# Moving four weight-remainder splits from VectorE to GpSimd, and re-ordering the depthwise convolution on VectorE

## The chip, the cores and the metric

The kernel runs on one core of a Trainium2 chip. The metric is the device time of one execution in microseconds; the table below gives the median of three.

## The reference, cut to what matters

A four-layer model (retention, conformer convolution, stick-breaking attention, retention, each followed by a squared-ReLU MLP) feeds a two-layer hybrid model, on one sequence of 256 tokens with 1024 channels in float32. Two stages matter here.

The conformer mixer, once in the program:

```
h = rms_norm(x)                               # 256 x 1024
a, b = split(h @ pw1_w + pw1_b)               # two halves of 1024
u = a * sigmoid(b)                            # the gated product
y[t, c] = dw_b[c] + sum_m dw_w[m, c] * u[t - 30 + m, c]     # 31 taps per channel
y = silu(layer_norm(y)) @ pw2_w + pw2_b ;  x = x + y
```

The attention of a hybrid layer, twice in the program: 16 heads of 64, scores over 256 keys with a bias, a softmax with a sink, probabilities times values, then `@ w_attn_out`, gates, and `@ w_o`.

## The kernel before, in words

Channels lie on partitions: a 256 x 1024 activation is 8 tiles of 128 x 256. Every product with a weight is made of three TensorE products (`three`, L679): the operand is split into a rounded part `hi` and the remainder `lo`, and hi*hi, hi*lo and lo*hi are summed. Weights stream from memory in units of 128 x 4096 (1 MB), 404 pieces of half a unit in all, through two buffers each of `raw`, `w_hi` and `w_lo` (unit u uses buffer u % 2). For each piece ScalarE rounds `w_hi <- raw` (L1099), VectorE computes `w_lo <- raw - w_hi` (L1507), and TensorE waits for `lo_done`. The helpers `ahead` and `next_unit` on both engines call these splits one unit ahead of use. SyncE loads unit u into `raw[u % 2]` once unit u - 2 is split (`lo_done`).

Each engine runs its own program in written order, and semaphores tie them together.

The conformer uses units 32 to 37. Units 32 to 35 give the two halves of pw1: one unit gives one PSUM pair with two tiles of `a` (columns 0 to 511) and two of `b` (columns 512 to 1023). ScalarE copies the `a` tiles with their bias into `C_U` (L1287) and writes sigmoid of the `b` tiles to `C_GATE` (L1290); that releases the PSUM pair. VectorE multiplies two tiles at once in place (`gated`, L1833). The depthwise convolution has eight tiles. VectorE makes tiles 0, 1, 2, 4 and 6: one scalar_tensor_tensor per tap, `y = u_shifted * w + y`, of 128 x 256 (L1795 for the tile pairs 0/1 and 2/4; L1813 for tile 6, which alternates between two accumulators and adds them at the end, L1818). TensorE makes tiles 3, 5 and 7 as 31 matmuls each with diagonal matrices (L869), which GpSimd builds (`diagonals`, L581: 62 of them early, the last 31 after `w_hi` of unit 35 has begun, because they lie in a buffer that is busy until then). Then TensorE takes the mean and the variance over channels (L888, L894), and units 36 and 37 are pw2.

The order on VectorE inside a convolution uses `link_late`: an instruction signals `vec`, and the next one waits only for the one before the last. Its elsewhere-used sister `link` waits for the instruction itself.

In a hybrid layer's attention, for each of 8 head groups VectorE adds the bias to scores (L2043), takes a maximum (L2049), and, after ScalarE's exponentials (L1443), normalises (L2060); TensorE transposes (L1033), ScalarE evacuates (L1449), TensorE multiplies with the values (L1042), VectorE evacuates (L1879). GpSimd fetches the bias tiles by DMA as `released` allows. The unit whose split this change touches there is the first of `w_attn_out`, called ATTN_OUT below; ScalarE rounds it at `j == 6`, VectorE subtracts it before `outputs(7)`.

Of the kernel before, what the change touches and what calls it, by code (L numbers as in the profile page):

```python
# [314 lines left out]
def build_program(nc, stream, columns, x_in, rows, tables, rel_bias, bias_rows, scratch, out):  # L315
# [6 lines left out]
    with ctx:  # L322
# [60 lines left out]
        conv_gated = sem("conv_gated")  # L383
# [60 lines left out]
        C_GATE = tiles(gate[:].rearrange("p b n -> p (b n)"))  # L444
# [33 lines left out]
        TABLES_BIAS, TABLES_RET, TABLES_CONV, TABLES_SB, TABLES_HYBRID = 6, (6, 16), 7, 12, (18, 20)  # L478
        CONV_FIRST = 16 + 2 * FFN1_CHUNKS
# [55 lines left out]
        def _(pool):  # L535
# [47 lines left out]

            retention(0)
# [12 lines left out]
            pool.wait_ge(hi_done, 2 * (CONV_FIRST + 3) + 1)  # L597
            diagonals(2)
            region_free()
# [43 lines left out]
        def _(pe):  # L643
# [215 lines left out]
            def conformer():  # L859
                convolved = {}  # L860

                def convolve(n):
# [3 lines left out]
                    pe.wait_ge(conv_gated, k // 2 + 1)  # L866
# [8 lines left out]
                unit_f(middle=turn_first)  # L875
                unit_f()
                convolve(0)
                unit_f()
                convolve(1)
                convolve(2)  # L880
# [208 lines left out]
        def _(act):  # L1089
# [184 lines left out]
            def conformer():  # L1274
# [7 lines left out]
                for i in range(4):  # L1282
                    o, done, slot = result(i == 0)
                    if i == 0:
                        act.wait_ge(zeroed, ZEROED_CONV)
                    for t in range(2):
                        run(C_U[:, 2 * i + t, TAPS - 1:UW], o[:, SEQ * t:SEQ * (t + 1)], ACT.Identity,  # L1287
                            bias=colv("pw1_b", 2 * i + t))
                    for t in range(2):
                        last = run(C_GATE[:, 2 * i + t, :], o[:, 512 + SEQ * t:512 + SEQ * (t + 1)],  # L1290
                                   ACT.Sigmoid, bias=colv("pw1_b", KT + 2 * i + t))
                    last.then_inc(done, 1)
# [96 lines left out]
            def hybrid(layer):  # L1389
# [65 lines left out]
                for j in range(8):  # L1455
# [3 lines left out]
                    if j == 6:  # L1459
# [38 lines left out]
        def _(dve):  # L1498
# [278 lines left out]
            def conformer(layer):  # L1777
                def link_late(ins):

                    ins.then_inc(vec, 1)  # L1780
                    dve.wait_ge(vec, S.due("vec") - 1)

                def convolve(first, second, between={}):

                    for m in range(TAPS):
                        if m in between:
                            between[m]()
                        for k in (first, second):
                            if m == TAPS - 1 and k == second:
                                dve.wait_ge(vec, S.seen["vec"])  # L1790
# [11 lines left out]
                def convolve_one(k):  # L1802

                    for m in range(TAPS):
                        dst = C_Y[:, k, :] if m % 2 == 0 else C_M
# [8 lines left out]
                        if m < TAPS - 1:  # L1814
                            link_late(ins)
                        else:
# [3 lines left out]
                def gated(i):  # L1820

                    if i == 0:
                        ahead(S.u + 1)
                        S.u += 1
                        ahead(S.u + 1)
                        use(False)
                    else:
                        ahead(S.u + 1)
                        S.u += 1
                        use()  # L1830
                    await_drained(S.p - 1)
                    two = slice(2 * i, 2 * i + 2)
                    tt(C_U[:, two, TAPS - 1:UW], C_U[:, two, TAPS - 1:UW], C_GATE[:, two, :],  # L1833
                       ALU.mult).then_inc(conv_gated, 1)
                    dve.wait_ge(conv_gated, i + 1)
                    if i == 2:
                        use(False)

                gated(0)
# [13 lines left out]
                ahead(CONV_FIRST + 4)  # L1853
# [10 lines left out]
                ahead(CONV_FIRST + 5)  # L1864
                S.u += 2
                add_bias(C_B)

# [84 lines left out]
            def hybrid(layer):  # L1952
# [126 lines left out]
                ahead(S.u + 1)  # L2079
# [3 lines left out]
                S.u += 1  # L2083
                rest_hid(4)
                for i in range(2):
# [57 lines left out]
```

## Time and profile before

| | us |
|---|---|
| median of 3 runs | 2527.19 (2526.38 to 2528.08) |
| the profiled execution | 2527.19 |
| its span, first to last instruction | 2525.4 |
| TensorE busy | 2416.1 (96%) |
| VectorE busy | 1500.9 (59%) |
| ScalarE busy | 1141.8 (45%) |
| GpSimd busy | 147.4 (6%) |

Rows of a timeline begin with the start in us from the span's start, then the time from the first start to the last end of the merged instructions, the engine, the line, the operation, output and inputs with shapes, and the count; brackets hold the idle time just before and who ended it. DVE is VectorE, ACT ScalarE, POOL GpSimd, PE TensorE.

### The profile page before, as it was taken

The numbers are of one execution on the slowest core, as the hardware profiler recorded it, in microseconds if no ns is written. First come the engines' busy times: TensorE is split into PE (matmuls) and PEld (weight loads), VectorE is DVE, ScalarE is ACT, GpSimd is POOL, SyncE is SP. The second block draws the span as 40 slices with busy tenths as digits, with TensorE's granted clock in tenths as the row PEclk, the third lists the DMA queues.
The fourth block names the chain that finished last, engine by engine and source line by source line (L and its number), as shares of the span: only waits on it lengthen the run. The fifth ranks groups of instructions, "written<-read, shape, count | busy, mean of one in ns | idle before, by whom it ended". The sixth has DMA issues, their size and how long they took to land.

```text
span 2525.4 us, 35292 instructions
## 1 busy us (share of the span) xinstructions
PE 2416.1 (96%) x14772; PEld 2157.7 (85%) x14772; DVE 1500.9 (59%) x1481; ACT 1141.8 (45%) x1127; POOL 147.4 (6%) x189
## 2 busy tenths in 40 slices
PE   7999999979999899999999999998999999989998
PEld 6787998869987789877789889998899899978997
DVE  6666556955466665586665565466644564586454
ACT  5444444144447654364444434354433443454443
POOL 0000170410000000000000000000000000010000
PEclk9999999989999999999999999999999999999999
DMA  6444654124544154545364434352454444423443
GB/s 255 175 183 173 231 202 168 67 83 193 199 166 167 67 192 173 197 163 188 142 238 179 183 143 194 151 192 80 163 200 195 179 176 175 176 94 136 193 167 123
DMA packets 68434, 424.38 MB, mean 168 GB/s; under 512 B 10848, under 2 KB 11136, under 8 KB 22496
## 3 DMA queue, kind: packets, MB, share of 16 engines
q1 hardware_dynamic: 58752, 399.83, 40.9%
q0 software_dynamic: 9568, 22.90, 2.9%
q8 instruction: 87, 1.43, 0.2%
q14 instruction: 27, 0.22, 0.0%
HBM read 421.60 MB, written 5.28 MB: 169 GB/s over the span
## 4 chain that ended last, share of the span: by engine, by line
PE 86%; DVE 8%; ACT 3%; issue 1%; DMA 0%; POOL 0%; DVEq 0%; ACTq 0%; POOLq 0%
PE pair L680 18%; PE pair L682 18%; PE pair L681 18%; PE acc L680 9%; PE acc L681 9%; PE acc L682 9%; DVE work L1795 2%; PE pair L717 1%; DVE w_lo L1507 1%; PE pair L1042 1%; DVE work L2043 1%; ACT work L1166 1%; PE pair L984 1%; DVE small L2049 1%; ACT act_hi L1148 0%
## 5 line engine op out<-in xcount | busy, mean ns | idle before, releaser
L1507 DVE TENSOR_TENSOR w_lo<-raw,w_hi 128x2048 fp32r<-128x2048 f32 (+1 forms) x404 | 859.7, 2163 | 258.1 <-ACT w_hi L1099 257.1
L1099 ACT ACTIVATE w_hi<-raw 128x2048 fp32r<-128x2048 f32 (+1 forms) x404 | 713.0, 1806 | 152.8 <-PE acc L682 132.6
L680 PE MATMUL pair<-act_hi,w_hi 128*128 128x256 f32 x2496 | 708.5, 284 | 2.5 <-DVE w_lo L1507 2.5
L682 PE MATMUL pair<-act_hi,w_lo 128*128 128x256 f32 x2496 | 706.3, 283 | 0.0
L681 PE MATMUL pair<-act_lo,w_hi 128*128 128x256 f32 x2496 | 706.3, 283 | 0.0
L680 PEld LDWEIGHTS pair<-act_hi,w_hi 128*128 128x128 f32 x2496 | 478.9, 192 | 5.2 <-issue 2.8
L681 PEld LDWEIGHTS pair<-act_lo,w_hi 128*128 128x128 f32 x2496 | 478.9, 192 | 2.3
L682 PEld LDWEIGHTS pair<-act_hi,w_lo 128*128 128x128 f32 x2496 | 478.8, 192 | 0.0
L680 PE MATMUL acc<-w_hi,hid_hi 128*128 128x512 f32 x848 | 334.7, 395 | 4.9 <-DVE hid_lo L1560 4.9
L681 PE MATMUL acc<-w_lo,hid_hi 128*128 128x512 f32 x848 | 331.0, 390 | 0.0
L682 PE MATMUL acc<-w_hi,hid_lo 128*128 128x512 f32 x848 | 330.5, 390 | 0.0
L680 PE MATMUL pair<-w_hi,act_hi 128*128 128x512 f32 (+1 forms) x576 | 225.8, 392 | 10.4 <-DVE w_lo L1507 6.3
L682 PE MATMUL pair<-w_hi,act_lo 128*128 128x512 f32 (+1 forms) x576 | 222.1, 386 | 0.0
L681 PE MATMUL pair<-w_lo,act_hi 128*128 128x512 f32 (+1 forms) x576 | 221.9, 385 | 0.0
L680 PEld LDWEIGHTS acc<-w_hi,hid_hi 128*128 128x128 f32 x848 | 159.8, 188 | 38.1 <-DVE hid_lo L1560 5.4
L682 PEld LDWEIGHTS acc<-w_hi,hid_lo 128*128 128x128 f32 x848 | 159.6, 188 | 33.9
L681 PEld LDWEIGHTS acc<-w_lo,hid_hi 128*128 128x128 f32 x848 | 159.9, 189 | 32.3 <-issue 1.4
L1650 DVE TENSOR_TENSOR val<-gate 128x1024 f32<-128x1024 f32 x32 | 39.3, 1227 | 210.2 <-ACT gate L1195 210.2
L1195 ACT ACTIVATE gate<-pair 128x1024 f32<-128x1024 f32 x32 | 32.9, 1027 | 247.5 <-PE pair L682 239.5
L680 PEld LDWEIGHTS pair<-w_hi,act_hi 128*128 128x128 f32 x576 | 109.0, 189 | 36.0 <-issue 9.9
L682 PEld LDWEIGHTS pair<-w_hi,act_lo 128*128 128x128 f32 x576 | 108.8, 189 | 21.9
L681 PEld LDWEIGHTS pair<-w_lo,act_hi 128*128 128x128 f32 x576 | 109.0, 189 | 21.3 <-issue 0.7
(212 smaller groups left out, 2588.0 us busy)
## 6 DMA issues: line engine op xcount, KB each, us to landing
raw<-weights SPq DMA_DIRECT2D x356, 1024.0 KB, 6.7
raw<-weights SPq DMA_DIRECT2D x48, 512.0 KB, 6.3
work<-bias_scratch POOLq DMA_DIRECT2D x32, 192.0 KB, 3.6
bias_scratch<-bias_rows POOLq DMA_DIRECT2D x4, 1024.0 KB, 22.6
work<-ret_gn_w POOLq DMA_DIRECT2D x8, 256.0 KB, 5.4
work<-ret_gn_b POOLq DMA_DIRECT2D x8, 256.0 KB, 5.8
work<-table_pool POOLq DMA_DIRECT2D x2, 1024.0 KB, 5.6
work<-table_decay POOLq DMA_DIRECT2D x2, 768.0 KB, 6.9
```

Of the source, the lines that this page charges most:

```text
L680: mm(o, a_hi, b_hi, start=start, stop=False)
L681: mm(o, a_hi, b_lo, start=False, stop=False)
L682: return mm(o, a_lo, b_hi, start=False, stop=stop)
L717: last = tr(o[:, P * k:P * (k + 1)], xs[:, a, P * k:P * (k + 1)], ident[:])
L984: last = mm(o[:, (k % 4) * SEQ:(k % 4 + 1) * SEQ], H_UP[:, s, k * P:(k + 1) * P], H_POOL[:, k // 2, s, :], start=s == 0, stop=s == 1)
L1042: last = mm(o[:, 512 * i:512 * i + SEQ], H_V[:, s, P * (j // 4):P * (j // 4) + P], H_PT[:, j % 2, i, s, :], start=s == 0, stop=s == 1)
L1099: run(w_hi[slot][:, part], raw[slot][:, part], ACT.Copy).then_inc(hi_done, 1)
L1166: run(xs[:, a, :], x[:, a, :], ACT.Square, scale=D ** -0.5, accum_out=ss[:, a:a + 1]).then_inc(ss_ready, 1)
L1195: run(gate[:, slot, :], o[:], ACT.Relu).then_inc(done, 1)
L1507: tt(w_lo[slot][:, part], raw[slot][:, part], w_hi[slot][:, part].bitcast(F32), ALU.subtract).then_inc(lo_done, 1)
L1650: tt(val[:, S.c % 2, :], gate[:, slot, :], gate[:, slot, :], ALU.mult).then_inc(value_ready, 1)
L1795: ins = stt(C_Y[:, k, :], C_U[:, k, m:m + SEQ], colv("dw_w", KT * m + k), C_Y[:, k, :], ALU.mult, ALU.add)
```

## The change

1. GpSimd gets `split_low`, the same subtraction as L1507, and runs it for units 35, 36 and 37 of the conformer (35 ahead of the last 31 diagonals, 36 and 37 behind them) and for ATTN_OUT in each hybrid layer (behind the last bias tile). VectorE drops these, and instead waits for `lo_done` at the end of the conformer and of the attention. On ScalarE the rounding of ATTN_OUT moves from `j == 6` to `j == 1`.
2. In the conformer ScalarE no longer copies the `a` tiles. VectorE makes the gated product straight from PSUM, one scalar_tensor_tensor per tile, `(a + bias) * gate`, and this now releases the PSUM pair. TensorE's diagonal convolutions wait for that release.
3. On VectorE tiles 0 and 1 are made one after the other with the two-accumulator form, tiles 2 and 4 as a pair, tile 6 as before; `link_late` goes, and the engine waits (`link`) for the second of every two instructions.

```diff
+            def split_low(u):
+                slot = u % 2
+                for piece in range(2):
+                    part = place_of(u, piece)
+                    pool.wait_ge(lo_done, 2 * u + piece)
+                    pool.wait_ge(hi_done, 2 * u + 1 + piece)
+                    nc.gpsimd.tensor_tensor(w_lo[slot][:, part], raw[slot][:, part], w_hi[slot][:, part].bitcast(F32),
+                                            ALU.subtract).then_inc(lo_done, 1)
...
-            pool.wait_ge(hi_done, 2 * (CONV_FIRST + 3) + 1)
+            split_low(CONV_FIRST + 3)
             diagonals(2)
+            split_low(CONV_FIRST + 4)
+            split_low(CONV_FIRST + 5)
...
                     bias_tile(j)
+                split_low(ATTN_OUT[layer])
...
-                    pe.wait_ge(conv_gated, k // 2 + 1)
+                    await_drained(unit_use)
...
-                    for t in range(2):
-                        run(C_U[:, 2 * i + t, TAPS - 1:UW], o[:, SEQ * t:SEQ * (t + 1)], ACT.Identity,
-                            bias=colv("pw1_b", 2 * i + t))
...
-                    if j == 6:
+                    if j == 1:
                         ahead(S.u + 1)
...
-                            if m < TAPS - 1:
-                                link_late(ins)
-                            else:
-                                ins.then_inc(conv_ready, 1)
+                        if m < TAPS - 1:
+                            link(ins)
+                        else:
+                            ins.then_inc(conv_ready, 2)
...
+                    for t in range(2):
+                        last = stt(C_U[:, 2 * i + t, TAPS - 1:UW], o[:, SEQ * t:SEQ * (t + 1)],
+                                   colv("pw1_b", 2 * i + t), gate[:, slot, SEQ * t:SEQ * (t + 1)], ALU.add, ALU.mult)
+                    last.then_inc(done, 1)
...
-                gated(0)
-                ahead(CONV_FIRST + 2)
-                convolve(0, 1, {12: lambda: gated(1), 13: lambda: ahead(CONV_FIRST + 3)})
-                gated(2)
-                convolve(2, 4, {10: lambda: gated(3)})
+                gated(0)
+                convolve_one(0)
+                gated(1)
+                convolve_one(1, lambda: gated(2))
+                convolve(2, 4, lambda: gated(3))
                 convolve_one(6)
...
-                ahead(S.u + 1)
                 outputs(7)
...
                 rest_hid(4)
+                dve.wait_ge(lo_done, 2 * S.split)
```

VectorE in the conformer, from the first gated product on, before (C_U, C_Y and the accumulators all lie in `work`):

```order
L1833 TENSOR_TENSOR work<-work,gate 128x2x256
L1792 TENSOR_SCALAR work<-work,cols 128x256 x2
L1795 SCALAR_TENSOR_TENSOR work<-work,cols 128x256 x22
L1833 TENSOR_TENSOR work<-work,gate 128x2x256
L1795 SCALAR_TENSOR_TENSOR work<-work,cols 128x256 x2
L1507 TENSOR_TENSOR w_lo<-raw,w_hi 128x2048 x2
L1795 SCALAR_TENSOR_TENSOR work<-work,cols 128x256 x36
L1833 TENSOR_TENSOR work<-work,gate 128x2x256
L1792 TENSOR_SCALAR work<-work,cols 128x256 x2
L1795 SCALAR_TENSOR_TENSOR work<-work,cols 128x256 x18
L1507 TENSOR_TENSOR w_lo<-raw,w_hi 128x2048 x2
L1833 TENSOR_TENSOR work<-work,gate 128x2x256
```

and now (line numbers of the changed kernel):

```order
L1832 SCALAR_TENSOR_TENSOR work<-pair,cols,gate 128x256 x2
L1815 TENSOR_SCALAR work<-work,cols 128x256
L1817 TENSOR_SCALAR work<-work,cols 128x256
L1819 SCALAR_TENSOR_TENSOR work<-work,cols 128x256 x29
L1822 TENSOR_TENSOR work<-work 128x256
L1832 SCALAR_TENSOR_TENSOR work<-pair,cols,gate 128x256 x2
L1815 TENSOR_SCALAR work<-work,cols 128x256
L1817 TENSOR_SCALAR work<-work,cols 128x256
L1819 SCALAR_TENSOR_TENSOR work<-work,cols 128x256 x14
L1832 SCALAR_TENSOR_TENSOR work<-pair,cols,gate 128x256 x2
L1819 SCALAR_TENSOR_TENSOR work<-work,cols 128x256 x15
L1822 TENSOR_TENSOR work<-work 128x256
```

The two pairs of `w_lo` subtractions are gone from between the taps, the gated products read the PSUM pair, and tiles 0 and 1 come one after the other.

GpSimd around the diagonals, before:

```order
L581 TENSOR_SCALAR work<-ident,cols 128x128 x83
L581 TENSOR_SCALAR val<-ident,cols 128x128 x10
L539 DMA work<-table_sb_mask 128x384
```

and now:

```order
L580 TENSOR_SCALAR work<-ident,cols 128x128 x62
L591 TENSOR_TENSOR w_lo<-raw,w_hi 128x2048 x2
L580 TENSOR_SCALAR work<-ident,cols 128x128 x21
L580 TENSOR_SCALAR val<-ident,cols 128x128 x10
L591 TENSOR_TENSOR w_lo<-raw,w_hi 128x2048 x4
L538 DMA work<-table_sb_mask 128x384
```

Six subtractions of 128 x 2048 come to this engine here, two ahead of the last 31 diagonals and four behind them.

## Rows read from the trace of the kernel before

**Rows 1.** The page's head: span, busy time of each engine.
```profile
span 2525.4 us, 35292 instructions
PE 2416.1 (96%) x14772; PEld 2157.7 (85%) x14772; DVE 1500.9 (59%) x1481; ACT 1141.8 (45%) x1127; POOL 147.4 (6%) x189
```

**Rows 2.** Chain that ended last, conformer: start us, us, what.
```profile
431.49 0.85 ACT gate L1290 x2
432.37 0.70 DVE work L1833
...
444.06 4.50 DVE w_lo L1507 x2
448.56 14.84 DVE work L1795 x36
...
472.30 4.40 DVE w_lo L1507 x2
...
494.64 11.49 DVE work L1813 x29
506.16 0.43 DVE work L1818
```

**Rows 3.** Timeline of VectorE, end of the conformer.
```profile
493.97 0.41 DVE L1809 TENSOR_SCALAR work<-work,cols 128x256 f32<-128x256 f32 x1
...
528.50 4.49 DVE L1507 TENSOR_TENSOR w_lo<-raw,w_hi 128x2048 fp32r<-128x2048 f32 x2
```

**Rows 4.** Timeline of VectorE, hybrid layer: the short convolution with `link`.
```profile
1488.22 0.62 DVE L1966 TENSOR_SCALAR work<-work,cols 128x256 f32<-128x256 f32 x2
1488.88 1.80 DVE L1968 SCALAR_TENSOR_TENSOR work<-work,cols 128x256 f32<-128x256 f32 x4
```

**Rows 5.** Timeline of ScalarE, conformer.
```profile
429.35 0.84 ACT L1287 ACTIVATE work<-pair,cols 128x256 f32<-128x256 f32 x2 [2.00 <-PE pair L799]
...
436.56 3.73 ACT L1099 ACTIVATE w_hi<-raw 128x2048 fp32r<-128x2048 f32 x2
...
484.91 0.48 ACT L1280 ACTIVATE work<-pair,cols 128x256 f32<-128x256 f32 x1 [8.22 <-PE pair L869]
498.30 0.48 ACT L1280 ACTIVATE work<-pair,cols 128x256 f32<-128x256 f32 x1 [12.91 <-PE pair L869]
```

**Rows 6.** The instructions of GpSimd's L581: duration ns min/median/max, first and last start.
```profile
L581 POOL TENSOR_SCALAR work<-ident,cols x83: 595/601/5034, 307.4 to 462.9; 128x128 f32<-128x128 f32 x83
```

**Rows 7.** Timeline of GpSimd and VectorE around one such meeting.
```profile
344.94 3.45 POOL L581 TENSOR_SCALAR work<-ident,cols 128x128 f32<-128x128 f32 x1
344.40 2.47 DVE L1507 TENSOR_TENSOR w_lo<-raw,w_hi 128x2048 fp32r<-128x2048 f32 x1 [0.49 <-ACT w_hi L1099]
331.97 2.29 DVE L1507 TENSOR_TENSOR w_lo<-raw,w_hi 128x2048 fp32r<-128x2048 f32 x1 [1.94 <-ACT w_hi L1099]
```

**Rows 8.** GpSimd by line and form: count, busy us, mean ns, idle before.
```profile
L546 POOL MEMSET work<- 64x2048 f32 x6 | 10.9, 1809 | 513.6 <-DVE small L1578 513.4
```

**Rows 9.** Timeline of GpSimd, conformer.
```profile
438.58 25.21 POOL L581 TENSOR_SCALAR work<-ident,cols 128x128 f32<-128x128 f32 x21 [73.86 <-ACT w_hi L1099]
463.78 8.48 POOL L581 TENSOR_SCALAR val<-ident,cols 128x128 f32<-128x128 f32 x10
```

**Rows 10.** Timelines of GpSimd and VectorE, first hybrid layer's attention.
```profile
1713.16 1.07 POOL L539 DMA_DIRECT2D work<-bias_scratch  x2 [4.42 <-DVE small L1578]
1714.71 0.18 DVE L2059 RECIPROCAL small<-small 128x4 f32<-128x4 f32 x1
1714.92 1.23 DVE L2060 TENSOR_TENSOR work<-work,small 128x1024 f32<-128x1024 f32 x1
1719.52 0.16 DVE L2050 TENSOR_TENSOR small<-small,work 128x4 f32<-128x4 f32 x1
1735.85 4.49 DVE L1507 TENSOR_TENSOR w_lo<-raw,w_hi 128x2048 fp32r<-128x2048 f32 x2
```

**Rows 11.** Waits between 1694 and 1750 us: who for whom, us, times, longest.
```profile
PE pair L1033 <- DVE work L2060: 7.2, 5, 2.7
PE pair L680 <- issue: 1.2, 1, 1.2
```

More of the change, by code:

```diff
@@ L382, in build_program @@
         conv_ready = sem("conv_ready")
-        conv_gated = sem("conv_gated")
         centred = sem("centred")
@@ L443, in build_program @@
         C_Y, C_SQ = tiles(work[:, 2304:4352]), tiles(work[:, 0:2048])
-        C_GATE = tiles(gate[:].rearrange("p b n -> p (b n)"))
         C_MEAN = work[:, 6400:6528]
@@ L478, in build_program @@
         TABLES_BIAS, TABLES_RET, TABLES_CONV, TABLES_SB, TABLES_HYBRID = 6, (6, 16), 7, 12, (18, 20)
+        ATTN_OUT = [n_units - 2 * FFN2_CHUNKS * (2 - layer) - HYBRID_UNITS * (1 - layer) - 4 for layer in range(2)]
         CONV_FIRST = 16 + 2 * FFN1_CHUNKS
@@ L875, in conformer @@
                 unit_f(middle=turn_first)
+                use_1 = S.p - 1
                 unit_f()
-                convolve(0)
+                use_2 = S.p - 1
+                convolve(0, use_1)
                 unit_f()
-                convolve(1)
-                convolve(2)
+                use_3 = S.p - 1
+                convolve(1, use_2)
+                convolve(2, use_3)
                 o = open_pair()
@@ L1283, in conformer @@
                     o, done, slot = result(i == 0)
-                    if i == 0:
-                        act.wait_ge(zeroed, ZEROED_CONV)
                     for t in range(2):
-                        run(C_U[:, 2 * i + t, TAPS - 1:UW], o[:, SEQ * t:SEQ * (t + 1)], ACT.Identity,
-                            bias=colv("pw1_b", 2 * i + t))
-                    for t in range(2):
-                        last = run(C_GATE[:, 2 * i + t, :], o[:, 512 + SEQ * t:512 + SEQ * (t + 1)],
+                        last = run(gate[:, slot, SEQ * t:SEQ * (t + 1)], o[:, 512 + SEQ * t:512 + SEQ * (t + 1)],
                                    ACT.Sigmoid, bias=colv("pw1_b", KT + 2 * i + t))
-                    last.then_inc(done, 1)
+                    last.then_inc(gate_ready, 1)
                     if i == 2:
@@ L1777, in conformer, with convolve @@
             def conformer(layer):
[L1778 to L1783, printed above, removed]
+                def convolve(first, second, middle):
                     for m in range(TAPS):
-                        if m in between:
-                            between[m]()
+                        if m == 26:
+                            middle()
                         for k in (first, second):
-                            if m == TAPS - 1 and k == second:
-                                dve.wait_ge(vec, S.seen["vec"])
                             if m == 0:
@@ L1796, in convolve, with convolve_one @@
                                           C_Y[:, k, :], ALU.mult, ALU.add)
-                            if m < TAPS - 1:
-                                link_late(ins)
-                            else:
-                                ins.then_inc(conv_ready, 1)
-                def convolve_one(k):
+                        if m < TAPS - 1:
+                            link(ins)
+                        else:
+                            ins.then_inc(conv_ready, 2)
+                def convolve_one(k, middle=None):
                     for m in range(TAPS):
+                        if m == 16 and middle is not None:
+                            middle()
                         dst = C_Y[:, k, :] if m % 2 == 0 else C_M
@@ L1813, in convolve_one @@
                             ins = stt(dst, src, w, dst, ALU.mult, ALU.add)
-                        if m < TAPS - 1:
-                            link_late(ins)
-                        else:
+                        if m % 2 or m == TAPS - 1:
                             link(ins)
@@ L1820, in gated @@
                 def gated(i):
+                    o, done, slot = result(i == 0)
                     if i == 0:
-                        ahead(S.u + 1)
[L1824 to L1830, printed above, removed]
+                        S.split += 3
+                    S.g += 1
+                    dve.wait_ge(gate_ready, S.g)
+                    for t in range(2):
+                        last = stt(C_U[:, 2 * i + t, TAPS - 1:UW], o[:, SEQ * t:SEQ * (t + 1)],
+                                   colv("pw1_b", 2 * i + t), gate[:, slot, SEQ * t:SEQ * (t + 1)], ALU.add, ALU.mult)
+                    last.then_inc(done, 1)
                     await_drained(S.p - 1)
[L1832 to L1835, printed above, removed]
                     if i == 2:
                         use(False)
+                dve.wait_ge(zeroed, ZEROED_CONV)
                 gated(0)
-                ahead(CONV_FIRST + 2)
-                convolve(0, 1, {12: lambda: gated(1), 13: lambda: ahead(CONV_FIRST + 3)})
-                gated(2)
-                convolve(2, 4, {10: lambda: gated(3)})
+                convolve_one(0)
+                gated(1)
+                convolve_one(1, lambda: gated(2))
+                convolve(2, 4, lambda: gated(3))
                 convolve_one(6)
@@ L1852, in conformer @@
                 release_centred()
-                ahead(CONV_FIRST + 4)
                 o, done = fetch_pair()
@@ L2078, in hybrid @@
                 outputs(6)
-                ahead(S.u + 1)
                 outputs(7)
@@ L2083, in hybrid @@
                 S.u += 1
+                S.split += 1
                 rest_hid(4)
+                dve.wait_ge(lo_done, 2 * S.split)
                 for i in range(2):
```

3 lines of the change are left out of this document (1 added, 2 removed).

## The prediction

> **What bounds the kernel now.** I read the page's head first: TensorE is busy 96% of a span of 2525.4 us and VectorE 59% [rows 1]. So work taken from VectorE gains only where TensorE waits for VectorE. The chain of waits says where the changed code is such a place. In the conformer the chain leaves TensorE when ScalarE ends the first sigmoids and stays on VectorE from 432.37 to 506.59 us: gated products, taps, and the two pairs of `w_lo` subtractions that stand between the taps [rows 2]. There every microsecond on VectorE is one of the kernel. TensorE's own last diagonal convolution has ended when ScalarE evacuates it at 498.30 [rows 5], 8 us ahead of VectorE. In the attention of the hybrid layers TensorE waits five times for VectorE's normalisation, 7.2 us in one layer [rows 11]; so up to about 1730 us VectorE is the path there too.
>
> **The change on VectorE and ScalarE alone.** Four terms, all in the conformer.
>
> (a) ScalarE's two copies ahead of the first sigmoids took 0.84 us [rows 5]; without them the first gated product starts so much earlier: -0.8.
>
> (b) Four gated products took 0.70 us each with a gap of about 0.03 [rows 2]: 2.9. Now each is two scalar_tensor_tensors of 128 x 256. The linked pair of the hybrid layer is the nearest row: four in two linked pairs take 1.80 us [rows 4]. One instruction lasts 0.48 and its neighbour starts 0.40 behind it (11.49 us for 29, [rows 2]), so a pair lasts 0.88 and the next pair starts at 1.80 - 0.88 = 0.92. Four at 0.92 are 3.7: +0.8. The PSUM source may cost some hundredths.
>
> (c) Two pairs of subtractions leave the path: -(4.50 + 4.40) = -8.9 [rows 2]. The third pair, at 528.50 [rows 3], lies beside the matmuls of unit 36, which run until unit 37 is wanted, and is worth nothing.
>
> (d) The links. Before, 36 taps took 14.84, 0.412 each, and 29 took 11.49, 0.396 each [rows 2]. Tiles 0, 1, 2 and 4 are 120 taps and 4 first products: 120 x 0.41 + 1.4 = 50.6. Tile 6 runs from 493.97 to 506.59 [rows 2, 3]: 12.6. Together 63.2. Now a pair costs 0.92 for two taps. A single tile is 0.66 for its two tensor_scalars (1488.22 to 1488.88, [rows 4]), 14 pairs, one lone linked tap at 0.52 and the final addition at 0.43: 14.5. Three such are 43.5. Tiles 2 and 4 are 0.66 + 30 x 0.92 = 28.3. Together 71.8: +8.6.
>
> The sum of (a) to (d) is -0.3: what the subtractions give back, the waits take. Here the Trainium skill says otherwise. Its page "VectorE: DVE Perf Modes", section "The DRAIN you can't avoid", holds that a semaphore after each of a chain of operations costs nothing extra. This trace does not agree: 0.92 for a linked pair against 2 x 0.40 without the close wait [rows 2, 4]. By that rule (d) would be only the two additions, +0.9, and the sum -8.0.
>
> Does anything else become late? TensorE's convolutions now start after VectorE's gated products 1, 2 and 3. Without further delays product 1 comes at 431.5 + 0.9 + 14.5 = 447, product 3 at about 487, and the last diagonal convolution, 13.4 us long (484.91 to 498.30, [rows 5]), would end near 501, 6 us ahead of VectorE. The diagonals it needs end at 472.3 before [rows 9] and some 9 us later now, still ahead of 487.
>
> **The subtractions on GpSimd.** No row shows a GpSimd subtraction, so I bound it. Below: a memset of 2048 columns, one stream, is 1.81 us [rows 8]. Above: a tensor_scalar of 128 columns has a median of 0.60 [rows 6], and sixteen of them are 9.6. The memset is the nearer row, since start-up weighs most in a short instruction. If the two reads share one way in, it is 2 x 1.8 = 3.6; with the write not overlapped 5.4. I take the middle, 4.5.
>
> The Trainium skill has this very operation in "GPSIMD Engine Reference", section "Performance versus the Vector engine": 4497 ns for a tensor_tensor of 2048 float32. No run here shows it yet; the sum would be the same.
>
> The question is what VectorE does meanwhile. A GpSimd tensor_scalar of 0.60 us has a maximum of 5.03 [rows 6]. One took 3.45, from 344.94 on, while VectorE ran the subtraction that starts at 344.40 and the one behind it [rows 7]. So GpSimd stands still for whole VectorE instructions that read two operands from SBUF. It goes the other way as well: this VectorE subtraction took 2.47 against 2.29 for one on its own [rows 7]. That is 0.18 us, about what reading 128 columns takes. It looks as if the two engines take turns by instruction, not by element. If so, GpSimd's 2048 columns hold VectorE for nearly their whole length, and the taps, which read `C_U` and the accumulator, are stopped. Close waits leave VectorE without an instruction at the end of each pair, so GpSimd gets its turn within a microsecond.
>
> The rule in the Trainium skill is the same: "SBUF — State Buffer", section "Who interferes with whom", says that whoever comes first, VectorE with two SBUF inputs or GpSimd reading SBUF, has the shared ports for the whole instruction. The rows on which I rely are those above.
>
> (e) Conformer: 4.5 less the 0.2 that VectorE has free between pairs is 4.3 for each of 6 pieces: +25.8. All six fall on the path. ScalarE has the halves of unit 35 ready about 437.5 and 439.5 ([rows 5], less what it saves), so GpSimd subtracts in tile 0. The diagonals follow: 33.7 us before, one 4.5 us standstill in it [rows 9]; now 29. So units 36 and 37 come between about 477 and 496, in tiles 2 and 4. VectorE then ends near 506.6 - 0.3 + 25.8 = 532, and the last diagonal convolution, held by product 3, near 528 to 530, a slower clock after its wait counted in.
>
> (f) Attention, twice. GpSimd's last bias fetch is issued by 1714.2 [rows 10], and the first piece begins reading near 1714.7, in the reciprocal (one input) just ahead of the normalisation, which reads two SBUF operands [rows 10]. That waits 4.2. The second piece gets its turn after it, at about 1720.3, runs beside a copy and an addition that read PSUM and a reduction of one input (about 3.4 us), and holds the next small tensor_tensor about 1.1: together 5.3. Two layers: +10.6. The bounds are 2.1 (both pieces after a normalisation) and 8.6 (both ahead) a layer. Dropping VectorE's pair at 1735.85 [rows 10] gives nothing: TensorE is then in a weight unit and next waits 1.2 us for a PSUM buffer [rows 11]. Rounding earlier on ScalarE delays one group of exponentials by 3.4 us, which VectorE wants 4 us later: nothing.
>
> Sum: -0.3 + 25.8 + 10.6 = +36.1. The profiled execution took 2527.2 us, 1.8 more than its span and equal to the median, so the forecast is 2563. With the bounds of 1.8 and 9.6 for a piece, (e) runs from +9.6 to +56, and the whole from about 2538 to 2600; close to the middle I hold 3.8 to 5.4 a piece, 2554 to 2575 for this case.
>
> **Rivals.**
>
> *Shared by element.* VectorE's second operand gets every other turn while GpSimd reads. A tap reads 256 columns in some 0.28 of its 0.40 us (2048 take 2.2, [rows 2]); at half speed a pair goes from 0.92 to about 1.45, and a piece costs about 2.2. Conformer +13, attention +3: 2543. For it: the 0.18 is small. Against: GpSimd got nothing for 3 and 5 us, which sharing would not do.
>
> *VectorE always goes first.* GpSimd fills the gaps and VectorE loses only what it lost to the diagonals, 0.412 against 0.396 a tap. This ends on the other side, not slower: -0.3 + 1 = 2528. The place is the taps; it decides as long as a piece, stretched to about 10 us, still lets the diagonals end by 488 and unit 37 be split by 533. For it: 36 taps beside diagonals lost only 0.6 us [rows 2]. Against: a diagonal reads only 128 columns, so it fits in a gap, and the 0.18.
>
> *Links for nothing*, as by the skill's rule, and no stop: 2527.2 - 8.0 = 2519. The row of 1.80 speaks against it [rows 4].
>
> *A much longer GpSimd piece*, near the upper bound, with stops: 2590 or more.
>
> **How the numbers follow.** Stopped for whole instructions: 0.60, at 2563. Shared: 0.18, at 2543. VectorE first: 0.17, at 2528. Links for nothing: 0.03. Long piece: 0.02. The first case lies likeliest, so 2563. Stretching the first case by half its own width again and taking in the second, but leaving out the other three, gives 2531 to 2584 for 8 in 10. A measurement here tells 0.2%, 5 us, from no change. Faster: 0.03; within it: 0.15, nearly all of "VectorE first"; slower: 0.82.
>
> **What would show it.** Taps that read SBUF stretched from 0.48 to over 4 us, six times in the conformer and about twice in each attention, would show (e) and (f). GpSimd's L591 near 4.5 us would show the price. Linked pairs at 0.92 show (d). TensorE idle between its second and third diagonal convolution shows what waits. If taps stay at 0.48 during L591, I am wrong, and the time is near 2528; if they come to 0.7 or 0.8, it is sharing.

## The result and the profile after

The changed kernel takes 2570.20 us (median of 4 runs, 2569.77 to 2570.93) against 2527.64 (4 runs, 2526.38 to 2528.29): ratio 1.0169, 95% interval 1.0151 to 1.0187. It is 42.6 us slower. The forecast was +36.1. The head of the profile's page, to be held against [rows 1]:

```profile
span 2569.0 us, 35304 instructions
PE 2421.5 (94%) x14772; PEld 2162.4 (84%) x14772; DVE 1530.4 (60%) x1477; ACT 1137.2 (44%) x1119; POOL 180.5 (7%) x199
```

The span grew by 43.6 us and TensorE's busy time by only 5.4, so TensorE waits more. VectorE is busy 29.5 us longer although ten subtractions of 2.3 us have left it: what grew is the length of other instructions. GpSimd's subtraction and VectorE's taps, by line (duration in ns, least, median, most; first and last start):

```profile
L591 POOL TENSOR_TENSOR w_lo<-raw,w_hi x10: 4508/4617/4883, 437.6 to 2279.7; 128x2048 fp32r<-128x2048 f32 x10
...
L1819 DVE SCALAR_TENSOR_TENSOR work<-work,cols x87: 472/485/4816, 431.6 to 531.5; 128x256 f32<-128x256 f32 x87
...
L1799 DVE SCALAR_TENSOR_TENSOR work<-work,cols x60: 471/484/4824, 472.6 to 517.5; 128x256 f32<-128x256 f32 x60
```

A tap's median is what it was, and its longest is as long as a whole GpSimd instruction. The timeline of VectorE in the conformer (answers [rows 2, 3]; L1832 gated product, L1819 and L1799 taps, L1822 addition):

```profile
429.95 0.88 DVE L1832 SCALAR_TENSOR_TENSOR work<-pair,cols,gate 128x256 f32<-128x256 f32 x2
...
431.58 22.43 DVE L1819 SCALAR_TENSOR_TENSOR work<-work,cols 128x256 f32<-128x256 f32 x29
...
456.26 7.02 DVE L1819 SCALAR_TENSOR_TENSOR work<-work,cols 128x256 f32<-128x256 f32 x14
...
464.22 7.25 DVE L1819 SCALAR_TENSOR_TENSOR work<-work,cols 128x256 f32<-128x256 f32 x15
...
472.62 39.89 DVE L1799 SCALAR_TENSOR_TENSOR work<-work,cols 128x256 f32<-128x256 f32 x50
...
531.98 0.42 DVE L1822 TENSOR_TENSOR work<-work 128x256 f32<-128x256 f32 x1
```

Tile 1's 29 taps take 14.3 us (7.02 for 14 and 7.25 for 15); tile 0's, with the same work, take 22.4. The 50 taps at 472.62 would be 23 us at 0.92 a pair and take 39.9. GpSimd in the same stretch (answers [rows 9]):

```profile
437.56 9.62 POOL L591 TENSOR_TENSOR w_lo<-raw,w_hi 128x2048 fp32r<-128x2048 f32 x2 [73.14 <-ACT w_hi L1115]
447.16 14.07 POOL L580 TENSOR_SCALAR work<-ident,cols 128x128 f32<-128x128 f32 x21
...
473.19 9.55 POOL L591 TENSOR_TENSOR w_lo<-raw,w_hi 128x2048 fp32r<-128x2048 f32 x2 [5.42 <-ACT w_hi L1115]
485.05 9.37 POOL L591 TENSOR_TENSOR w_lo<-raw,w_hi 128x2048 fp32r<-128x2048 f32 x2 [2.31 <-ACT w_hi L1115]
```

The six pieces lie exactly where the taps are long. The chain of waits puts them side by side, pair by pair:

```profile
437.07 0.89 DVE work L1819 x2
...
437.99 9.48 DVE work L1819 x2
...
447.50 0.89 DVE work L1819 x2
...
484.88 5.17 DVE work L1799 x2
490.08 5.03 DVE work L1799 x2
```

One pair holds both pieces of unit 35: its first tap waits for the first piece, its second for the second. VectorE's convolution ends at 532.40 instead of 506.59, and pw2 starts at 549.95 instead of 525.57: +24.4.

In each attention both pieces meet VectorE's smallest operations (answers [rows 10]):

```profile
1738.65 4.75 DVE L2050 TENSOR_TENSOR small<-small,work 128x4 f32<-128x4 f32 x1
1743.44 0.17 DVE L2051 TENSOR_SCALAR small<-small 128x4 f32<-128x4 f32 x1
1743.64 4.34 DVE L2052 TENSOR_TENSOR small<-work,small 128x4 f32<-128x4 f32 x1
```

```profile
1737.78 1.07 POOL L538 DMA_DIRECT2D work<-bias_scratch  x2 [4.42 <-DVE small L1589]
1738.86 9.10 POOL L591 TENSOR_TENSOR w_lo<-raw,w_hi 128x2048 fp32r<-128x2048 f32 x2
```

L2050 and L2052 read two operands from SBUF each. An operation of 4 columns that takes 0.16 us [rows 10] takes 4.75. L2051 between them reads one operand and takes its usual time; but it starts at 1743.44, just as the second piece does (1743.45), so it may simply have slipped in between. TensorE's waits in the two stretches (432 to 560 us, and 1725 to 1775, which answers [rows 11]):

```profile
PE pair L882 <- DVE work L1832: 27.2, 2, 17.9
```

```profile
PE pair L1049 <- DVE work L2060: 12.6, 3, 9.7
```

The 27.2 us are idle time of TensorE at its diagonal convolutions, which wait for VectorE's gated products. It costs nothing by itself: the last of them is evacuated at 528.80, 3.6 us ahead of VectorE's end. The 9.7 are on the path.

Where the 43.6 us of span arose can be read from the same instruction in both traces, by how much later it starts: +24.4 at pw2; +34.3 at VectorE's last `hid_lo` subtraction of the first hybrid attention (L1571 at 1778.70, against 1744.41), so 9.9 there; +43.7 at that of the second (2315.40 against 2271.74), so 9.4 there.

### The profile page after: what moved, and what is told of

The parts are those of the page before. It is cut to its first block, busy times and chain, and to the rows that moved or that the text cites. A ratio compares the mean times of both kernels' runs of the same rounds, so it can differ in the third digit from the quotient of the medians.

```text
span 2569.0 us, 35304 instructions
## 1 busy us (share of the span) xinstructions
PE 2421.5 (94%) x14772; PEld 2162.4 (84%) x14772; DVE 1530.4 (60%) x1477; ACT 1137.2 (44%) x1119; POOL 180.5 (7%) x199
## 4 chain that ended last, share of the span: by engine, by line
PE 86%; DVE 10%; ACT 3%; issue 1%; DMA 0%; POOL 0%; DVEq 0%; ACTq 0%
PE pair L693 18%; PE pair L695 17%; PE pair L694 17%; PE acc L693 9%; PE acc L694 9%; PE acc L695 9%; DVE work L1819 2%; DVE work L1799 2%; PE pair L730 1%; PE pair L1058 1%; PE acc L1037 1%; ACT work L1182 1%; PE pair L1000 1%; DVE work L2043 1%; ACT act_hi L1164 0%
## 5 line engine op out<-in xcount | busy, mean ns | idle before, releaser
L1518 DVE TENSOR_TENSOR w_lo<-raw,w_hi 128x2048 fp32r<-128x2048 f32 (+1 forms) x394 | 836.8, 2158 | 262.9 <-ACT w_hi L1115 261.9
L693 PE MATMUL pair<-w_hi,act_hi 128*128 128x512 f32 (+1 forms) x576 | 225.4, 391 | 10.6 <-DVE w_lo L1518 6.3
```

Of the source, the lines that this page charges most:

```text
L693: mm(o, a_hi, b_hi, start=start, stop=False)
L1518: tt(w_lo[slot][:, part], raw[slot][:, part], w_hi[slot][:, part].bitcast(F32), ALU.subtract).then_inc(lo_done, 1)
```

## The experiments

Unless it says otherwise each kernel is the one before with the edit shown. "VectorE's end" is the end of its convolution, 506.59 us before. Each trace reaches the conformer up to 0.9 us earlier or later than the trace before, for reasons ahead of the changed code; so where VectorE's ends are compared for a price, the start of its first gated product (432.37 before) is subtracted first. In the kernel before this stretch is 74.2 us long, 9.0 of it the two pairs of subtractions.

### Which part costs

**Only the conformer's subtractions on GpSimd**, with taps, links and gated products as before.

```diff
+            split_low(CONV_FIRST + 3)
             diagonals(2)
+            split_low(CONV_FIRST + 4)
+            split_low(CONV_FIRST + 5)
```

> The kernel before with one edit: units 35, 36 and 37 of the conformer are subtracted on GpSimd. Whole instructions are held: two pairs of VectorE's subtractions leave the path (-8.9) and six pieces stop the taps for about 4.5 us each (+27): +18, about 2546 us. Shared by element: -8.9 + 13, about 2532. VectorE first: -8, about 2520. If GpSimd finds no turn between taps that are waited for late, its pieces come only at other gaps, and the gain of 8.9 shows.

2545.56 us (2544.26 to 2546.38) against 2527.34: ratio 1.0071, interval 1.0055 to 1.0086. VectorE's end is 522.77, 91.0 us behind the start of its first gated product (431.76). Without the subtractions the stretch would be 65.2, so six pieces cost 25.8, 4.3 each.

```profile
L590 POOL TENSOR_TENSOR w_lo<-raw,w_hi x6: 4519/4580/8967, 438.0 to 491.5; 128x2048 fp32r<-128x2048 f32 x6
```

```profile
441.85 0.68 DVE L1845 TENSOR_TENSOR work<-work,gate 128x512 f32<-128x512 f32 x1
442.56 4.71 DVE L1806 SCALAR_TENSOR_TENSOR work<-work,cols 128x256 f32<-128x256 f32 x1
```

Here the first piece lasts 8.97 us. From 438.03 on VectorE ran taps back to back under `link_late` and none was held; only when it came out of the gated product, which is waited for, was the tap at 442.56 held, for 4.2 us. The kernel before shows the same at this place: a diagonal that starts at 438.58 lasts 5.03 us. It isn't so for every piece among such taps: the one that starts at 477.62 holds the tap beside it at once. What decides whether GpSimd gets its turn stays open.

**Only the attention's subtraction on GpSimd**, with ScalarE's rounding at `j == 1`.

> The kernel before with one edit: the first unit of w_attn_out is subtracted on GpSimd and rounded at j == 1, in both hybrid layers. Held, with both pieces ahead of the normalisation as the changed kernel's profile shows: 2 x 8.8 = +17.5, about 2545 us. Held with only one such piece a layer (the prediction's choice): +10.6, 2538. Not held: 2528.

2546.75 us (2545.92 to 2547.62) against 2527.34: ratio 1.0076, interval 1.0061 to 1.0092; +19.4 for two layers.

**The whole change with all subtractions back on VectorE**, in the conformer one pair among the taps of tile 0 and one ahead of the last gated product, and with ScalarE's rounding back at `j == 6`.

> The changed kernel with every subtraction back on VectorE; what stays is the gated product from PSUM and the tiles waited for in pairs. Links cost as the 1.80 us row says: -2.4 for the earlier start, +0.8 for the products, +8.6 for the links: +7, about 2534.5 us. A semaphore after an operation costs nothing: -0.7, about 2527.

2534.77 us (2533.96 to 2537.00): ratio 1.0030, interval 1.0018 to 1.0042. VectorE's end is 515.36. So +7.4, +17.0 for the subtractions' move in the conformer (532.40 less 515.36) and +19.4 in the attention make 43.8, where 42.6 was measured. Most of the difference is TensorE's variance: its 16 matmuls took 6.66 us in this kernel's trace and 5.38 in the changed kernel's.

**Only the close waits.**

```diff
-                            if m < TAPS - 1:
-                                link_late(ins)
-                            else:
-                                ins.then_inc(conv_ready, 1)
+                        if m < TAPS - 1:
+                            link(ins)
+                        else:
+                            ins.then_inc(conv_ready, 2)
```

(and in tile 6 `link` after every second tap).

> The kernel before with one edit: the late wait becomes a wait for the second of every two taps; the order of work stays. Links cost: 60 pairs from 0.82 to 0.92 and 14 from 0.79 to 0.92: +7.8, about 2535.4 us. A semaphore costs nothing: 2527.6.

2537.91 us (2536.95 to 2538.00) against 2527.34: ratio 1.0039, interval 1.0025 to 1.0053. VectorE's end is 516.6, 10 later. The loss is 10.6 us where 7.8 was expected.

```profile
450.68 17.52 DVE L1793 SCALAR_TENSOR_TENSOR work<-work,cols 128x256 f32<-128x256 f32 x36
...
482.99 19.21 DVE L1793 SCALAR_TENSOR_TENSOR work<-work,cols 128x256 f32<-128x256 f32 x42
```

The last pair without its wait taken off, the 42 taps are (19.21 - 0.88) / 20 = 0.92 a pair, as forecast; the 36, most of them beside GpSimd's diagonals, (17.52 - 0.88) / 17 = 0.98. Before it was 14.84 for 36 [rows 2], 0.82 a pair. So beside diagonals a pair with a close wait costs another 0.06. The section "The DRAIN you can't avoid" of "VectorE: DVE Perf Modes" in the Trainium skill, by which a semaphore after each operation costs nothing extra, does not hold for these taps.

### What holds VectorE

**GpSimd only writes**: six memsets of 128 x 2048 into an idle buffer at the places of the six pieces; the subtractions stay on VectorE.

```diff
+                    nc.gpsimd.memset(hid_lo, 0.0)   # x6, same places as the six pieces
```

> The kernel before; GpSimd runs a memset of 128 x 2048 (which reads nothing) into a dead buffer at the six places where the changed kernel subtracts. It adds work and no result. Only instructions that read SBUF on GpSimd hold VectorE: 0, about 2527.6 us. Any long GpSimd instruction holds VectorE: 6 x 1.6 = +10, 2537.

2527.81 us (2526.00 to 2530.61, 10 runs) against 2528.22 (21 runs of the kernel before): ratio 0.9999, interval 0.9990 to 1.0009.

```profile
438.69 3.74 POOL L590 MEMSET hid_lo<- 128x2048 f32 x2 [73.84 <-ACT w_hi L1109]
...
472.33 7.57 POOL L590 MEMSET hid_lo<- 128x2048 f32 x4
```

```profile
477.47 16.71 DVE L1805 SCALAR_TENSOR_TENSOR work<-work,cols 128x256 f32<-128x256 f32 x42
```

Memsets are running from 472.33 to 479.90, the 42 taps begin in them at 477.47, and they take no longer than in the kernel before (16.72). Writing on GpSimd doesn't hold them.

**GpSimd reads one operand**: the same with a tensor_scalar of 128 x 2048.

```diff
+                    nc.gpsimd.tensor_scalar(hid_lo, hid_hi, 1.0, None, ALU.mult)   # x6
```

> As write_only, with a tensor_scalar of 128 x 2048 that reads one tensor. Held while GpSimd reads: its duration less 0.2, six times; at 2 to 3 us each +11 to +17, 2538 to 2545. Held only by two inputs on GpSimd: 2527.6.

2549.15 us (2546.19 to 2550.70) against 2528.22: ratio 1.0080, interval 1.0064 to 1.0095. That is +21, above all that was expected.

```profile
484.36 5.36 POOL L590 TENSOR_SCALAR hid_lo<-hid_hi 128x2048 fp32r<-128x2048 f32 x1
489.88 5.59 POOL L590 TENSOR_SCALAR hid_lo<-hid_hi 128x2048 fp32r<-128x2048 f32 x1 [0.16 <-POOL hid_lo L590]
```

```profile
L1805 DVE SCALAR_TENSOR_TENSOR work<-work,cols x120: 471/473/3912, 433.6 to 513.8; 128x256 f32<-128x256 f32 x120
```

```profile
483.95 30.27 DVE L1805 SCALAR_TENSOR_TENSOR work<-work,cols 128x256 f32<-128x256 f32 x42
```

One operand takes GpSimd longer than two (5.4 to 5.6 us in the last four against 4.6; the first two, which met VectorE in the middle of its work, took 9.79 and 6.21), and a tap is held at most 3.4 us of it (3.91 less 0.47). The 42 taps, with four such instructions beside them, lose 30.27 - 16.72 = 13.6 us, 3.4 each, and VectorE's end is 20.2 later for six. So reading is what holds, also with one operand, though for a part of the length only: each of the four held taps ends 1.45 us before the GpSimd instruction beside it, and the next taps, which read two operands, run in that rest at their usual length. What GpSimd does in it stays open. Three of the four also began in the middle of back-to-back taps under `link_late` (489.88, 495.63, 501.38) and held the next tap 0.29 us later; so the missing close wait isn't what kept the piece at 438.03 out.

**The same subtractions in eight short ones** of 256 columns each, against the first experiment.

```diff
-                    nc.gpsimd.tensor_tensor(w_lo[slot][:, part], ...)
+                    for c in range(part.start, part.stop, 256):
+                        cs = slice(c, c + 256)
+                        ins = nc.gpsimd.tensor_tensor(w_lo[slot][:, cs], ...)
```

> As the run pool_conf, but each GpSimd subtraction of 2048 columns is cut into eight of 256. Held by instruction: each of the eight reads for about 0.55 us, and VectorE has some 0.2 of that free between taps and gets its turn in GpSimd's start-up time, so a piece stops it about 2.8 us in place of 4.4: 8 to 10 us faster than pool_conf. Shared by element, or a fixed share of the port: the same columns cost the same, within 2 us of pool_conf.

2541.89 us (2541.47 to 2542.29): ratio 1.0053, interval 1.0037 to 1.0068; 3.7 below the median with long instructions (4.6 if each is held against the kernel before as measured beside it, 2528.22 and 2527.34), between the two expectations.

```profile
L593 POOL TENSOR_TENSOR w_lo<-raw,w_hi x48: 721/902/5105, 437.8 to 508.4; 128x256 fp32r<-128x256 f32 x48
```

```profile
L1815 DVE SCALAR_TENSOR_TENSOR work<-work,cols x120: 470/505/1012, 432.9 to 502.7; 128x256 f32<-128x256 f32 x120
```

The longest tap falls from 4.81 to 1.01 us: each stop becomes shorter with the GpSimd instruction. But there are eight times as many stops. From the first gated product (431.49) to VectorE's end (519.40) it is 87.9 us, so 2048 columns cost (87.9 - 65.2) / 6 = 3.8 instead of 4.3. What is short is the single stop, not their sum.

The same trace has two VectorE instructions that read one tensor from SBUF (the others are columns of scalars), beside GpSimd's short subtractions:

```profile
503.58 0.81 DVE L1829 TENSOR_SCALAR work<-work,cols 128x256 f32<-128x256 f32 x1
504.31 0.81 DVE L1831 TENSOR_SCALAR work<-work,cols 128x256 f32<-128x256 f32 x1
```

Before, the same two take 0.41 and 0.35 us. So one tensor operand instead of two does not by itself keep VectorE free.

**The attention's pieces where VectorE reads PSUM**: as the second experiment, with ScalarE's rounding left at `j == 6`.

```diff
-                    if j == 1:
+                    if j == 6:
                         ahead(S.u + 1)
```

> As pool_attn, but ScalarE rounds the unit at j == 6 as before, so that GpSimd subtracts from about 1732 us on, when VectorE's chain of normalisations has ended and its copies read PSUM only. Held by instruction, two-input VectorE work only: 0 to +0.5, about 2528. A cost that goes with the operation wherever it stands: +17, as pool_attn.

2528.36 us (2526.41 to 2529.94, 11 runs) against 2528.22: ratio 0.9999, interval 0.9990 to 1.0008.

```profile
1730.94 9.25 POOL L591 TENSOR_TENSOR w_lo<-raw,w_hi 128x2048 fp32r<-128x2048 f32 x2 [17.66 <-ACT w_hi L1110]
```

```profile
1731.06 0.86 DVE L1890 COPY val<-pair 64x256 f32<-64x256 f32 x2 [1.34 <-PE pair L1053]
1734.07 0.86 DVE L1890 COPY val<-pair 64x256 f32<-64x256 f32 x2 [2.15 <-PE pair L1053]
```

The same two pieces cost 19 us in two layers at one place and nothing 16 us later, where VectorE waits for TensorE or copies from PSUM to SBUF. Four copies run beside the first piece, at their usual 0.42 and 0.43 us each. So the edit that looks harmless, the rounding moved from `j == 6` to `j == 1`, is what makes the attention slow: it lets GpSimd's pieces start among the normalisations.

### What of the change is worth keeping

**Only the gated product from PSUM.**

```diff
+                        last = stt(C_U[:, 2 * i + t, TAPS - 1:UW], o[:, SEQ * t:SEQ * (t + 1)],
+                                   colv("pw1_b", 2 * i + t), gate[:, slot, SEQ * t:SEQ * (t + 1)], ALU.add, ALU.mult)
```

> The kernel before with the gated product from PSUM alone (no ScalarE copies, TensorE waits for the release). The first product starts 2.4 us earlier and the four products take 0.8 more: -1.6, about 2526. If the release by VectorE holds TensorE up: 2528 or more.

2526.48 us (2524.93 to 2530.68, 11 runs) against 2528.25 (27 runs): ratio 0.9994, interval 0.9985 to 1.0003. VectorE's end is 505.3; the time can't be told from no change.

**Only unit 36's subtractions later**, behind the centring pass, where VectorE waits for TensorE's variance.

```diff
-                        ahead(S.u + 1)
+                        if i < 3:
+                            ahead(S.u + 1)
```

> The kernel before with one edit: VectorE subtracts unit 36 after the centring, while TensorE makes the variance (VectorE waits 5.9 us there), not between the taps. The pair of 4.4 us leaves the path: -4.4, about 2523.2 us. If the variance's wait is too short or the unit's place in the weight stream matters: 2525 to 2528.

2523.49 us (2522.55 to 2526.47, 11 runs): ratio 0.9982, interval 0.9973 to 0.9991. Faster, within 0.2%.

```profile
473.54 0.69 DVE L1834 TENSOR_TENSOR work<-work,gate 128x512 f32<-128x512 f32 x1 [0.91 <-ACT gate L1290]
```

4.4 us left the path and the end moved by 3.1, to 503.50: 0.9 went into a wait for the sigmoids, and this trace was 0.3 late from the start.

**Both.**

> Both edits, gate and late36: -6, about 2521.6 us, if they add. TensorE's last diagonal convolution would then be within 2 us of VectorE's end and may take up to 1 us of it back.

2525.09 us (2522.87 to 2528.72, 11 runs): ratio 0.9990, interval 0.9981 to 0.9999. They don't add.

```profile
476.62 0.88 DVE L1827 SCALAR_TENSOR_TENSOR work<-pair,cols,gate 128x256 f32<-128x256 f32 x2 [6.13 <-ACT gate L1286]
```

```profile
462.38 0.58 PE L678 MATMUL pair<-act_hi,w_hi 128*128 128x256 f32 x1 [2.57 <-DVE work L1827]
```

VectorE now releases the PSUM pair. Its product for unit 34 came at 461.5, so TensorE began unit 35 2.6 us late and unit 35's sigmoids were late in turn; with nothing between, VectorE waited 6.1 us.

**Both, with the products earlier among the taps.**

```diff
-                convolve(0, 1, {12: lambda: gated(1), 13: lambda: ahead(CONV_FIRST + 3)})
-                gated(2)
-                convolve(2, 4, {10: lambda: gated(3)})
+                convolve(0, 1, {12: lambda: gated(1), 13: lambda: ahead(CONV_FIRST + 3), 24: lambda: gated(2)})
+                convolve(2, 4, {16: lambda: gated(3)})
```

> The kernel before with the change's gated products from PSUM, unit 36's centring subtractions put behind the centring pass, and the gated product of unit 34 moved forward among the taps of tiles 0 and 1 (after tap 24), that of unit 35 among those of tiles 2 and 4 (after tap 16). In the sum of the two edits VectorE waited 6.1 us for the gate before unit 36's gated product, because TensorE had waited 2.57 us at unit 35 for unit 34's product to leave its tiles. If the late release is the cause, both waits go: VectorE's convolution ends some 3 us earlier than with the subtractions' edit alone (503.5), near 500.5, pw2 starts as much earlier, and the time is about 2520.5 us. If TensorE's last diagonal convolution or ScalarE's sigmoids set the gate instead, a wait of 2 us or more stays before unit 36's product and the time is that of the subtractions' edit alone, 2523.5 us. Over 2526 us would mean that the products now wait in VectorE's queue for sigmoids not yet there and delay the taps.

2519.98 us (2516.81 to 2520.25, 7 runs) against 2526.55 (11 runs): ratio 0.9972, interval 0.9961 to 0.9984. It is the only kernel here whose median is lower by more than 0.2%. (Where the expectation says unit 36's gated product, it is that of unit 35.)

```profile
455.66 0.86 DVE L1827 SCALAR_TENSOR_TENSOR work<-pair,cols,gate 128x256 f32<-128x256 f32 x2
...
500.26 0.42 DVE L1814 TENSOR_TENSOR work<-work 128x256 f32<-128x256 f32 x1
```

Both waits are gone and VectorE ends at 500.68. TensorE is no longer idle between its last diagonal convolution and the mean, and in this execution keeps its clock at the variance. Two stretches show it, first of this kernel and then of the one before (us; busy time and instructions of PE, PEld, DVE, ACT, POOL; granted clock; DMA share; GB/s):

```profile
501.00:509.00 8.00, 4.56 (x20) 3.38 (x19) 7.05 (x6) 3.40 (x3) 0.00 (x0) 1.00 0.00 0
```

```profile
507.00:516.00 9.00, 6.51 (x16) 4.71 (x16) 2.41 (x3) 3.40 (x3) 0.00 (x0) 0.52 0.00 0
```

```profile
504.37 3.69 PE L895 MATMUL pair<-work 128*128 128x256 f32 x16 [2.49 <-ACT work L1296]
```

```profile
511.20 5.87 PE L894 MATMUL pair<-work 128*128 128x256 f32 x16 [2.49 <-ACT work L1300]
```

The variance's 16 matmuls take 3.69 us at 2.4 GHz (granted clock 1.00) and 5.87 near 1.2 GHz (0.52), where TensorE had been idle for 5.8 us ahead of the mean's last matmuls. The length of the idle time alone does not tell the price: with 1.0 to 2.4 us of it the variance of other kernels here took 5.16 to 6.66 us (the largest is that of the kernel with the subtractions back on VectorE, idle 0.99). So 5.9 us saved on VectorE became 8.4 at pw2 (517.15 against 525.57) in this execution, which is the fastest of the seven; the medians differ by 6.6.

## Why the prediction was right, and where a size was off

**The order of the cases.** Held for whole instructions (0.60) is what happened. *Shared by element* and *VectorE always first* wanted taps of 0.8 or 0.48 us beside L591; they are 4.8. *Links for nothing* wanted the close waits free; alone they cost 10.6 us. *A much longer piece* wanted far over 5 us; it is 4.6. The Trainium skill's figure of 4497 ns for GpSimd's tensor_tensor ("GPSIMD Engine Reference", "Performance versus the Vector engine") agrees with the least of ten, 4508, and its rule of the shared ports ("SBUF — State Buffer", "Who interferes with whom") with the 4.75 us of a 4-column operation and with the memsets that held nobody. The whole length of the instruction, as the prediction put it, is not what a one-operand instruction took: 3.4 us of 5.6.

**(a) Earlier start, booked -0.8, measured -2.1**: the first product starts at 429.95 instead of 432.37, 2.4 earlier, but TensorE's matmuls ahead of it had already ended 0.3 earlier. Besides the two copies (0.84), ScalarE's table load (1.28) left the path. With no copy to do first, ScalarE loads the sigmoids' table while TensorE still works:

```profile
427.03 1.28 ACT L1301 ACT_TABLE_LOAD   x1
429.01 0.84 ACT L1301 ACTIVATE gate<-pair,cols 128x256 f32<-128x256 f32 x2 [0.70 <-PE pair L812]
```

**(b) Four gated products, +0.8**: a pair takes 0.88 and the next instruction starts 0.92 behind it (429.95 to 430.87). Right.

**(c) Two pairs of subtractions off the path, -8.9**: in the kernel with them back on VectorE they take 4.49 and 4.50. Right.

**(d) Links, booked +8.6, measured +10.4**: without GpSimd's pieces VectorE takes 85.4 us from its first gated product to its end (429.95 to 515.36), with the subtractions still in it, against 74.2 before; 11.2 less the 0.8 of (b) is 10.4. Some 1.3 of the missing 1.8 are the pairs beside diagonals: there 14 taps took 7.00 us and without diagonals 6.38. The misses of (a) and (d) have opposite signs: (a) to (d) sum to +0.1 or +0.2 where -0.3 was booked, and this agreement is partly luck.

**(e) Six stops in the conformer, 4.3 each, +25.8**: 532.40 - (515.36 - 9.0) = 26.0, 4.3 each. The 4.5 us for a piece, the middle of 3.6 and 5.4, was close as well (median 4.6). But the sum behind it, one read of 1.8 us for each operand, is not borne out: with one operand GpSimd took longer, 5.4 to 5.6 us. Units 36 and 37 came between 473.19 and 494.42 (forecast 477 to 496), VectorE's end at 532.4 (forecast 532), TensorE's last diagonal convolution before it. That the places fit is partly luck. I had GpSimd come to unit 36 when its diagonals were done, 29 us behind unit 35. They took only 20.6 (447.16 to 467.77), and GpSimd then waited 5.42 us for ScalarE to round unit 36 and 2.31 for unit 37. Of the +25.8 of VectorE's end pw2 felt 24.4. TensorE was idle for only 1.1 us ahead of the mean's last four matmuls (5.8 before), which took 1.13 us instead of 2.08, and the variance took 5.38 instead of 5.87. The granted clock there was 0.81 where it had been 0.52, in the same columns as above:

```profile
532.50:541.50 9.00, 6.47 (x20) 4.77 (x20) 2.42 (x4) 3.40 (x3) 0.00 (x0) 0.81 0.00 0
```


**(f) Attention, booked 5.3 a layer, measured 8.8 in the two held operations (4.75 + 4.34 less twice 0.16), 9.9 and 9.4 by the starts at the attention's end.** This term failed in its size. I had the first piece start in the reciprocal and hold the normalisation, and the second behind the normalisation, beside work that reads PSUM. It started at 1738.86, right behind the last bias fetch (1737.78 + 1.07). That fetch is 24.6 later than before, so the piece starts at 1714.2 on the scale of before, 0.5 earlier than I placed it: I had put half a microsecond between the two. It held L2050, the 4-column operation behind the maximum (the two starts lie 0.2 us apart, and starts on GpSimd are rough). Then came the part that I had not reckoned with: while L2051 ran for 0.17 us the second piece got its turn, and it held L2052. Both pieces fell ahead of the normalisation, which was my upper bound (8.6). In this chain of small operations that wait for each other GpSimd found an opening behind the first, and how short an operation is did not protect it. The rest of the 9.9 and 9.4 is not traced in full; part of it is TensorE after its long wait, whose transposes take 1.97 us instead of 1.09:

```profile
1735.33 1.09 PE L1049 MATMUL pair<-ident,work 128*128 128x128 f32 x8 [0.45 <-DVE work L2060]
...
1749.58 1.97 PE L1049 MATMUL pair<-ident,work 128*128 128x128 f32 x8 [9.70 <-DVE work L2060]
```

The 6.5 us between forecast and result are so: held operations +7.0 (twice 3.5), what follows the waits in the attentions +1.7 (9.9 + 9.4 - 17.6), pw2 -1.1 (24.4 where (a) to (e) gave 25.5), and -1.1 because the medians lie 42.6 apart and these starts in the two traces 43.7.

## What to carry to other kernels

Before work is moved to GpSimd, list what VectorE executes at that time. Where its instructions read two operands from SBUF, a GpSimd subtraction of 4.6 us stopped them for nearly its own length, so 2.3 us saved on VectorE were paid for with 4.3. Place such work where VectorE reads PSUM or waits; the same two pieces cost 19 us or nothing by where ScalarE's rounding stood. One operand from SBUF on VectorE isn't shown to be safe: two tensor_scalars were stretched from 0.41 and 0.35 to 0.81 us. And before an engine is relieved at all, put the work where that engine waits anyway: one unit's subtractions in such a wait, with the gated products from PSUM placed by when TensorE wants its pair back, gave 6.6 us where the change lost 42.6.

## What the runs showed of the hardware that was not expected

- A one-operand tensor_scalar of 128 x 2048 float32 on GpSimd takes 5.4 to 5.6 us, longer than the two-operand subtraction (4.6), and holds a VectorE tap for about 3.4 us of it, until 1.45 us before its end.
- Eight instructions of 256 columns in place of one of 2048 cut the longest tap from 4.8 to 1.0 us, and the sum of the stops only from 4.3 to 3.8.
- Once in a trace, at 438.03, GpSimd's piece found no opening between back-to-back taps under `link_late` for 4.5 us (8.97 instead of 4.6), and VectorE lost nothing in that time. Later pieces among such taps got their turn within 0.3 us. What makes the difference stays open.
- Two VectorE tensor_scalars of 128 x 256 with one tensor operand took 0.81 us each beside GpSimd's subtractions of 256 columns, and 0.41 and 0.35 without.
- An ACT_TABLE_LOAD needn't wait for the data of the activation it serves: it ran 2 us ahead of the sigmoids (427.03 and 429.01).
